# Moving the key-pair copy, the prompt's compressed softmax and three sums of squares in a two-layer decoder step

## The reference

```python
h = rms_norm(x, g[i, 0]); m = mixer(h)          # conv in layer 0, attention in layer 1
x = x + rms_norm(m, g[i, 1])
x = x + rms_norm(square(relu(rms_norm(x, g[i, 2]) @ w1)) @ w2, g[i, 3])
x = x + sigmoid(x @ w_gate + b) * (p @ w_ple)

# attention: three branches, gated and added
kcc, vcc = compress(k), compress(v)             # windows of 32 keys, stride 16, a small MLP
pc = softmax(q @ kcc)                           # compressed branch
idx = top_k(pc summed into blocks of 64, 16)    # picks the selected blocks
o = g0 * (pc @ vcc) + g1 * attend(q_rot, selected) + g2 * attend(q_rot, last 512)
```

## Time and profile before

| what | value |
|---|---|
| device time, median of 3 runs | 1895.42 us (1894.66 to 1896.15) |
| the profiled execution, its own time | 1896.06 us |
| its span | 1894.2 us |
| PE busy | 1723.8 us, 91% of the span |
| DVE busy | 762.7 us, 40% |
| ACT busy | 616.7 us, 33% |
| POOL busy | 600.7 us, 32% |
| DMA | 180.08 MB, mean 95 GB/s |
| mean granted clock of PE | 0.954 of full speed |

### The profile page before, as it was taken

How to read it: one execution, slowest core, us unless ns; L and a number is a source line. 1 busy time by engine, 2 the same in 40 slices (tenths; PEclk the granted TensorE clock), 3 DMA queues, 4 the chain that set the end, 5 groups by cost and what they waited for, 6 DMA issues and landing times.

```text
span 1894.2 us, 31064 instructions
## 1 busy us (share of the span) xinstructions
PE 1723.8 (91%) x13247; PEld 1590.9 (84%) x13247; DVE 762.7 (40%) x1160; ACT 616.7 (33%) x970; POOL 600.7 (32%) x286
## 2 busy tenths in 40 slices
PE   5998989799999999989983666999979999999998
PEld 4997879799999999889983433565979999999978
DVE  5999932520212122460520734777252021212242
ACT  4210145432313132333220333676333231312232
POOL 3551222142333333123312000455413323333311
PEclk9998999899999999989996787999989999999999
DMA  7249611133322222112228184000212222122211
GB/s 238 90 117 140 190 60 75 67 134 134 108 98 85 90 70 87 67 67 80 89 65 263 60 250 135 2 2 2 102 45 78 80 89 90 68 89 90 86 48 73
DMA packets 61276, 180.08 MB, mean 95 GB/s; under 512 B 22851, under 2 KB 23763, under 8 KB 47251
## 3 DMA queue, kind: packets, MB, share of 16 engines
q1 hardware_dynamic: 60466, 177.18, 29.0%
q10 hardware_dynamic: 128, 0.88, 0.3%
q0 software_dynamic: 544, 0.03, 0.0%
HBM read 167.02 MB, written 16.45 MB: 97 GB/s over the span
## 4 chain that ended last, share of the span: by engine, by line
PE 81%; DVE 6%; SPq 4%; DMA 3%; ACT 2%; issue 2%; POOL 1%; ACTq 0%; DVEq 0%
PE ps L651 21%; PE ps L653 21%; PE ps L652 21%; PE ps L752 5%; PE ps L995 2%; PE ps L692 2%; PE ps L1023 2%; PE ps L1006 2%; POOL w_lo L573 1%; SPq L512 1%; SPq L484 1%; SPq L485 1%; DMA attn_t<-in_win 1%; PE ps L914 1%; PE ps L850 1%
## 5 line engine op out<-in xcount | busy, mean ns | idle before, releaser
L573 POOL TENSOR_TENSOR w_lo<-w_raw,w_hi 128x2048 fp32r<-128x2048 f32 x98 | 452.8, 4621 | 891.5 <-ACT w_hi L1063 891.5
L651 PE MATMUL ps<-ha,w_hi 128*128 128x288 f32 x1920 | 574.6, 299 | 32.4 <-DVE hb L1420 15.1
L652 PE MATMUL ps<-hb,w_hi 128*128 128x288 f32 x1920 | 572.0, 298 | 0.0
L653 PE MATMUL ps<-ha,w_lo 128*128 128x288 f32 x1920 | 571.9, 298 | 0.0
L651 PEld LDWEIGHTS ps<-ha,w_hi 128*128 128x128 f32 x1920 | 366.7, 191 | 36.9 <-issue 22.7
L652 PEld LDWEIGHTS ps<-hb,w_hi 128*128 128x128 f32 x1920 | 366.9, 191 | 0.0
L653 PEld LDWEIGHTS ps<-ha,w_lo 128*128 128x128 f32 x1920 | 366.6, 191 | 0.0
L651 PE MATMUL ps<-hid_hi,w_hi 128*128 128x288 f32 x1024 | 301.8, 295 | 0.0
L653 PE MATMUL ps<-hid_hi,w_lo 128*128 128x288 f32 x1024 | 301.6, 295 | 0.0
L652 PE MATMUL ps<-hid_lo,w_hi 128*128 128x288 f32 x1024 | 301.6, 295 | 0.0
L1063 ACT ACTIVATE w_hi<-w_raw 128x2048 fp32r<-128x2048 f32 x98 | 186.9, 1907 | 171.1 <-PE ps L653 165.1
(11 more groups left out here) (247 smaller groups left out, 1999.5 us busy)
## 6 DMA issues: line engine op xcount, KB each, us to landing
w_raw<-in_w SPq DMA_DIRECT2D x98, 1024.0 KB, 4.8
ring<-in_sel_pages SPq DMA_DIRECT2D x64, 256.0 KB, 3.4
ring<-in_cmp_pages SPq DMA_DIRECT2D x40, 256.0 KB, 3.4
attn_t<-in_win SPq DMA_DIRECT2D x16, 512.0 KB, 6.5
cmp_hb<-in_cmp_pages SPq DMA_DIRECT2D x16, 256.0 KB, 2.9
x<-in_x SPq DMA_DIRECT2D x4, 576.0 KB, 5.8
out_y<-x SPq DMA_DIRECT2D x8, 288.0 KB, 2.1
big<-in_cmp_pages SPq DMA_DIRECT2D x8, 256.0 KB, 3.0
```

Source lines behind the costliest of these rows:

```text
L573: nc.gpsimd.tensor_tensor(w_lo[j % 2][:, :], w_raw[:, k, :], w_hi[j % 2][:, :].bitcast(F32), ALU.subtract).then_inc(w_ready, 1)
L651: nc.tensor.matmul(to, wh, chunk(hi, k, a * HT, HT), start=k == 0, stop=False)
L652: nc.tensor.matmul(to, wh, chunk(lo, k, a * HT, HT), start=False, stop=False)
L653: return nc.tensor.matmul(to, wl, chunk(hi, k, a * HT, HT), start=False, stop=k == C - 1)
```

## The change

It does five things.

1. `kv_pairs` gets another place (in `w_raw`), and SP copies it once the last value block has been split, during the value tiles. `w1` moves one place up the ring and is loaded after the first half of the value tiles; the samples' compressed keys and values and the output of the rotated keys hang on it. The output of the values goes behind the pages of sample 2.
2. Page numbers: all 8 of a row are read into registers first, ahead of the waits for its place; then the 8 loads follow.
3. The samples' compressed scores are made before the prompt's compression, and `qbd` (the queries in block form) has a place of its own, zeroed earlier.
4. The prompt's compressed scores use banks 6, 4, 5, 7; their maxima and exponentials still come before the samples, but their sums, divisions and transposes move into the first four turns of the sample loop (`over_sum(b + 1)`, `prompt_probs(b)`, `probs_transposed(b)`).
5. Norms: norm 0 is summed by PE from 8 squared chunks (no DVE adds), and ACT splits the first weight block ahead of norm 0's root. In both MLPs the sums of squares stand inside the first two tiles, one chunk at a time. `post_norm` makes the low part of a chunk right after its addition to x. The norm factors of norms 2 and 6 go to a free tile slot.

The diff, cut to its core (waits and bank numbers of other places are left out):

```diff
+        BLOCKS += [("w1", 0), ("sel_pages", 0), ("win_k", 0), ("win_v", 0), ("win_k", 1), ("sel_pages", 1), ("win_v", 1),
+                   ("sel_pages", 2)]
...
+        w1 = at_byte("w1", [P, 2, 16, P], ring_byte + 4 * BLK)
+        kv_pairs = at_byte("kv_pairs", [P, 2, KV, SEQ], ring_byte)
...
+                if (src, row) == ("w1", 0):
+                    sp.wait_ge(w_ready, W_OF["out"])
+                    sp.wait_ge(act_freed, FREED[FIRST["kv_cmp"] + 3][1])
+                    for e in range(2):
+                        for later in range(2):
+                            sp.dma_start(kv_pairs[64 * later:64 * later + 64, :, e:e + 3:2, 0:SEQ - later].rearrange(
+                                             "p v g t -> p (v g) t"),
+                                         kv_cmp[64 * e:64 * e + 64, :, later:SEQ]).then_inc(pairs_in, 16)
+                    sp.dma_start(out["kv_cmp"], kv_cmp[:, :, :]).then_inc(kv_cmp_stored, 16)
+                if src.endswith("pages"):
+                    sp.wait_ge(pages_in, 16)
+                    numbers = [sp.value_load(pages[0:1, row * PAGES + j:row * PAGES + j + 1], min_val=0, max_val=POOL - 1)
+                               for j in range(PAGES)]
...
                 lo, k = PLACE[i]
+                if src == "sel_pages" and row == 1:
+                    sp.wait_ge(phid_mm, 2)
...
-                    for j in range(PAGES):
-                        page = sp.value_load(pages[0:1, row * PAGES + j:row * PAGES + j + 1], min_val=0, max_val=POOL - 1)
+                    for j, page in enumerate(numbers):
...
                 if (src, row) == ("w1", 0):
-                    sp.wait_ge(tile_done, FIRST["v_tok"] + 2 * TT)
-                    sp.wait_ge(act_freed, FREED[FIRST["v_tok"] + 2 * TT - 1][1])
...
                     sp.wait_ge(rot_done, 12)
                     sp.wait_ge(cmp_stored, 16 * 2)
                     sp.dma_start(k_cmp_s, k_kept.rearrange("p b (g c) -> p b g c", g=2)).then_inc(cmp_in, 16)
                     sp.dma_start(v_cmp_s, v_kept).then_inc(cmp_in, 16)
+                    sp.dma_start(out["k_rot"], k_rot[:, :, :]).then_inc(kept_out, 16)
...
                         if k == C - 1:
                             last.then_inc(tile_done, 1)
+                    if norm is not None:
+                        if k == 0:
+                            pe.wait_ge(std_ready, norm)
+                        pe.wait_ge(sq_ready, C * norm + k + 1)
+                        last = square_sums(mix[:, k, :], k == 0, k == C - 1)
                 if norm is not None:
-                    stats(norm)
+                    last.then_inc(sq_summed, 1)
...
+            def square_sums(src, first, end):
+                for i in range(4):
+                    last = nc.tensor.matmul(STAT_Q[32 * i:32 * i + 32, :], tab("mean")[:, 0:32],
+                                            src[:, QT * i:QT * (i + 1)], start=first, stop=end)
+                return last
...
+            def prompt_probs(n):
+                to = t_slot(("prompt", n, 0))
+                pe.wait_ge(pc_ready, n + 2)
+                for j in range(4):
+                    last = nc.tensor.transpose(to[:, 128 * j:128 * j + 128], pc[n][:, 128 * j:128 * j + 128], tab("ident"))
+                last.then_inc(t_mm, 1)
...
                 if b >= 1:
-                    finish_s(b - 1, t_group(b, 4))
+                    finish_s(b - 1)
+                if b < PT:
+                    prompt_probs(b)
...
+            split_weight(0)
             act.wait_ge(consts_in, 32)
             std(0)
-            split_weight(0)
...
-            for m in range(C):
-                add_square(0, m)
...
             less_max(0)
+            block_queries(q_rot)
             over_sum(0)
-            less_max(1)
-            less_max(2)
-            over_sum(1)
             dropped_blocks()
-            over_sum(2)
-            less_max(3)
-            less_max(4)
-            over_sum(3)
-            over_sum(4)
-            block_queries(q_rot)
+            for n in range(1, PT + 1):
+                less_max(n)
...
             for b in range(NB):
+                if b < PT:
+                    over_sum(b + 1)
                 if b + 1 < NB:
                     scores_out(b + 1)
```

More of the change, by code:

```diff
@@ L165 @@
     LOADED.append(_at[_sem])
-DIRECT = (3, 7)
+DIRECT, MLP_NORM = (0, 3, 7), (3, 7)
 def adds(n):
@@ L183 @@
 PER_C = 2 * PT
-def t_group(b, k):
-    return 5 * b + k - (b > 0)
+T_GROUPS = []
+for _b in range(NB):
+    T_GROUPS += [("probs", _b, _k) for _k in range(4)] + [("rows", _b - 1, 0)] * (_b > 0) + [("prompt", _b, 0)] * (_b < PT)
+T_GROUPS.append(("rows", NB - 1, 0))
+T_AT = {g: i for i, g in enumerate(T_GROUPS)}
+PHID_BANK = (6, 0)
+CMP_BANK = (6, 4, 5, 7)
 def program(nc, ext, out):
@@ L604, in _ @@
             split_weights(C + 1, W_OF["out"])
+            pool.wait_ge(tile_done, FIRST["gates"] + 1)
+            nc.gpsimd.memset(qbd[:, :, :, :, :], 0.0).then_inc(qbd_zero, 1)
             pool.wait_ge(rot_done, 12)
@@ L843, in _ @@
             last.then_inc(tile_done, 1)
+            pe.wait_ge(cmp_in, 16 * 2)
+            pe.wait_ge(qbd_ready, 1)
+            for b in range(NB):
+                for g in range(2):
+                    last = nc.tensor.matmul(ps[64 * g:64 * g + 64, 7, 64 * b:64 * b + 64],
+                                            qbd[:, b, g, :, :].rearrange("p e m -> p (e m)"), k_cmp_s[:, b, g, :],
+                                            start=True, stop=True)
+            last.then_inc(sc_mm, 1)
             block_there(B_OF["w1", 0])
@@ L921, in scores_s, with t_slot @@
                 last.then_inc(s_mm, 1)
-            def t_slot(n):
+            def t_slot(group):
+                n = T_AT[group]
                 if n >= 2:
-                    b, k = [(b, k) for b in range(NB + 1) for k in range(5) if (b, k) != (0, 4)][n - 2]
-                    if k == 4:
-                        pe.wait_ge(t_fin, b)
+                    kind, b, k = T_GROUPS[n - 2]
+                    if kind == "rows":
+                        pe.wait_ge(t_fin, b + 1)
+                    elif kind == "prompt":
+                        pe.wait_ge(ct_out, b + 2)
                     else:
```

218 lines of the change are left out of this document (106 added, 112 removed).

## The result

The changed kernel takes **1830.7 us** (median of 4 runs, 1830.3 to 1838.4); the kernel before took 1895.0 beside it (1885.0 to 1896.2). The ratio is **0.968, with a 95% interval of 0.965 to 0.970**. The forecast was 1827, range 1812 to 1845. The profiled execution took 1830.6 us, its span is 1828.8 (before 1896.1 and 1894.2).

What follows compares the result with a forecast made beforehand. The prediction took PE, busy for 91% of the span, as the bound outside a few places. Savings of 63 (middle), 3 (start) and 2 (MLPs), 68 to 69 us, gave 1895.4 - 68.5 = 1827 us, range 1812 to 1845.

Steps and rivals of the forecast that it cites:

- The pairs' wait goes, the samples' compressed keys are late next: Before the sample loop: pairs copied by 983; samples' compressed keys and values arrive at 994, a new 4 us wait.
- Before the loop -52.5: Middle before the sample loop: DVE takes over sample 0's scores at 1023.7 instead of 1076.2, 52.5 us less.
- Page period 0.55: Sample loop: SP's page period falls from 1.10 to 0.55 us, shortening the loop by 11.6 us.
- `over_sum` in the turns +2.3: Sample loop: the prompt's sums moved into its first four turns add 2.3 us, between 0 and 15.
- The tail after sample 7's scores stays 18.2: End of the sample loop: what follows sample 7's scores stays 18.2 us, until the prompt's attention.
- The start -3: Kernel start: first product at 21.1 instead of 24.15, 3 us less, bounds 0 and 4.
- Page numbers in the convolution stage 0: Convolution stage: eight reads and eight issues take 8.8 us as before, change 0, bounds -3 and 3.
- The MLPs -1 per layer: Both MLPs: sums stand where PE waits for DVE's low parts, 1 us less per layer, 2 together.
- B: Rival for the sample loop: loads stay the pace, the loop gains nothing net, 1840 us; chance 0.2.
- C: Rival before the loop: slow queue, arrival at 1000, or sample 2's pages late by 5; 1835 us; chance 0.1.
- D: Rival for the sample loop: loads vanish behind work, 9 us per sample from sample 3 on; 1814 us; chance 0.13.
- E: Rival for the prompt's attention: PE granted the lower clock, slower than before, up to 1977 us; chance 0.02.

Runs made afterwards that it cites:

- e9_pairs_late: Changed kernel, but SP waits for the last value tile before issuing the key pairs' copies and all behind them in its order: 1851.9 us.
- e6_sums_behind: Changed kernel, but in the sample loop's turns DVE makes the prompt's sums behind the next sample's scores_out instead of ahead: 1842.4 us.
- e7_kept_first: Changed kernel, but the samples' compressed keys and values load right behind the pairs, ahead of w1 and the 1.2 MB compressed-key output: 1825.2 us.
- e1_block: Changed kernel, but the MLP norms' sums of squares stand in one block behind the first two tiles' chunks again; new post_norm order kept: 1838.3 us.
- e9_keys_only: Changed kernel, but from sample 3 on only the keys' half of each selected page is loaded: 1827.8 us.
- e2_old_order: Changed kernel, but with DVE's old order in post_norm; the sums stay between the products: 1835.3 us.
- e8_block_and_old: Changed kernel, but with the MLP sums of squares in one block again and DVE's old post_norm order: 1828.9 us.
- e10_window_first: Changed kernel, but samples' compressed keys and values load right behind the pairs, and a sample's window keys ahead of its pages: 1818.0 us.
- e11_all: Changed kernel, but compressed keys and values right behind the pairs, window keys ahead of pages, MLP sums in one block, old post_norm order: 1818.2 us.
- e5_old_start: Changed kernel, but DVE adds norm 0's squares again and ACT's split of the first weight block stands behind the root: 1835.0 us.
- e4_before_numbers: Kernel before, with one edit alone: the eight page numbers are read ahead of the waits for the buffer: 1884.4 us.
- e3_one_by_one: Changed kernel, but SP reads each page number right before issuing that page again, behind the buffer wait: 1841.5 us.

## Why the prediction was right, and which term was not

- **The pairs' wait goes, the samples' compressed keys are late next:** right, arrival forecast at 994, measured 994.4. `e9_pairs_late` puts the price of a late start of this queue at 25 us of the middle.
- **Before the loop -52.5:** DVE's take-over at 1023.16 against a forecast of 1023.7. Less the 0.4 us won ahead of the middle it is -52.6. In it the order of the steps held too: block sums 1011.2, the four `less_max` 2.05 apart. (The prediction's own terms, 1011, 2.8 and four times 2.06, end at 1022.0 and not at 1022.5.)
- **Page period 0.55:** measured 0.52 in the row shown, 0.51 to 0.72 over the eight rows. From outputs to the scores three on 12.0, 13.0 and 12.2 us, against 12.3; from these to the next outputs 11.3 and 10.6, against 10. Worth of this part 13, against 11.6. (In the prediction 9.5 and 2.5 are 12.0, not 12.3, and three times 3.8 is 11.4.)
- **`over_sum` in the turns +2.3:** too high. From the scores of sample b+1 to the last row of outputs of sample b PE takes 8.4 us in turn 0, 8.0 before, and 8.5 in turn 1, 8.3 before: 0.4 and 0.2 where I had 0.3 and 1. In turn 2 DVE still waits for PE behind the sums, as forecast. My reasoning on its queue was incomplete: `e6_sums_behind` shows that the order on DVE is worth 9.9 us through PE, which I hadn't seen.
- **The tail after sample 7's scores stays 18.2:** it took 15.8, since those scores ran at the full clock (1.94 us against 3.68). That is more than the difference between 64.9 and 63: without it the middle would be 62.5 us shorter. In the total these 2.4 us made up for part of the MLPs' miss, and that was luck. Ahead of these scores PE had idled 1.6 us, where it idled 6.4 before; in `e7_kept_first` it idled 4.3, they ran at the lower clock again and the tail was 18.4. The tail was no fixed term: it hangs on the clock that PE has there.
- **The start -3:** right, -3.2, and by the mechanism forecast (subtraction outside POOL's split, reciprocal not held).
- **Page numbers in the convolution stage 0:** nothing to be told from its noise. The step "8.8 as before" doesn't fit, though: the row of pages issued at 161 us takes 4.5 us for eight, with the numbers read ahead, and took 9.5.
- **The MLPs -1 per layer: wrong, it is +2.0 per layer** (the bound for both together was +2, it is +4.0, or 3.2 should layer 0, too, have the 0.4 that the new order gives back). The step that failed is "now they stand where PE waits for DVE's low parts". I took DVE for the pace from its period of 2.12 us against 1.6 of PE. But PE begins at the low clock and falls behind: in the kernel before its eight chunks take 3.02, 2.56, 1.60, 1.60, 1.75, 1.70, 1.60 and 1.62 us (the last without the block), so it finds the later low parts ready, and its waiting in all of them is the 0.25 us over 1.60 in the fifth and sixth. Work put between the products of an engine that doesn't wait is paid in full, and here at 0.57 us a group, twice the 0.27 in a block. The second part, "one DVE instruction as cover in place of three", I had priced at 1 us; alone it would cost 2.5 (`e1_block`), hidden only because PE had become slower still.
- **Rivals.** B (loads stay the pace because reading costs as much in a block) fell with a period of 0.51 to 0.72, where over 0.9 would have been its sign. C fell with the arrival at 994. D fell: bytes still set the pace (`e9_keys_only`). E: the prompt's attention ran at the same granted clock, 0.96 over its 166 us, busy as in the earlier trace rows:

```profile
1108.00:1274.00 166.00, 157.94 (x1279) 97.12 (x1280) 120.06 (x266) 109.13 (x340) 89.82 (x130) 0.96 0.06 20
```

## What to carry to other kernels

To claim that an added piece of work fills a wait, find the wait in the engine's own rows: comparing the periods of two engines doesn't show it, since one that started late or at a low clock catches up for many rounds. Where a buffer's release starts a load, take everything out from behind that release that doesn't depend on it: numbers read ahead were worth 13 us, half a megabyte of window keys 4.5 more. And before work is moved behind other work on one engine, look in what order the other engines ask for its results.

## What the runs showed beyond this

- **Where the noise sits.** From the 33rd product with a first operand's high part to layer 0's first MLP product eight traces have the same program (all but those of the kernel before and of the experiments on page numbers and DVE's order), yet the stretch took 303.5 to 308.2 us. In it PE waits once for a compressed page:

```profile
PE ps L782 <- DMA ring<-in_cmp_pages: 3.8, 1, 3.8
```

In the other traces this wait is between 1.5 and 11.6 us. It stands behind 8 stores of the convolution's state, whose issue alone takes 20.5 us. So medians of different kernels differ by more than their edits explain (`e1_block`, `e2_old_order`), and single stretches were compared instead. That this one wait makes the spread isn't shown: `e7_kept_first` waited 9.2 us there and took 306.3, `e1_block` waited 5.1 and took 308.2.
- **Alternation between kinds of matmul has a price:** 0.30 us a group here (0.57 less 0.27), seen as PE time without idle time in brackets. Why was not tried.
- In the changed kernel PE stood for 3.4 us (at 1065.5) in the middle of a row of products that wait for nothing, beside full DMA queues. The same stop of 3.4 to 3.7 us, in the same row of products of one sample, is in the traces of six experiments: `e1_block`, `e2_old_order`, `e8_block_and_old`, `e9_pairs_late`, `e10_window_first` and `e11_all`. `e5_old_start` has one of 3.6 in the row ahead of it, `e4_before_numbers` one of 4.4. It isn't in `e7_kept_first`, in `e9_keys_only` (as expected there if it came from the load), in `e3_one_by_one` or in `e6_sums_behind`. One instruction packet landed within it in the changed kernel. A late fetch behind the loads would fit that, but `e7_kept_first` loads as much and has no stop; the cause is open.
